# Both down projections of an FFN block in 1 MB units with seven products, the first sum of weight blocks made by an accumulating DMA

## What is computed

```python
def swiglu(x, w_gate, w_up, w_down):
    return (jax.nn.silu(x @ w_gate) * (x @ w_up)) @ w_down

f = swiglu(rmsnorm(h, ffn1_pre_g[l]), ffn1_w_gate[l], ffn1_w_up[l], ffn1_w_down[l])
h = h + 0.5 * rmsnorm(f, ffn1_post_g[l])
```

## Time and profile before

| | us |
|---|---|
| median of 3 runs (1766.72 to 1767.81) | 1766.88 |
| the profiled execution | 1766.51 |
| its span, first to last instruction | 1764.7 |
| PE busy | 1738.4 |
| DVE busy | 1392.2 |
| ACT busy | 961.4 |
| POOL busy | 141.1 |

### The profile page before, as it was taken

How to read it: one execution, slowest core, us unless ns; L and a number is a source line. 1 busy time by engine, 2 the same in 40 slices (tenths; PEclk the granted TensorE clock), 3 DMA queues, 4 the chain that set the end, 5 groups by cost and what they waited for, 6 DMA issues and landing times.

```text
span 1764.7 us, 21449 instructions
## 1 busy us (share of the span) xinstructions
PE 1738.4 (99%) x7784; PEld 1430.1 (81%) x7784; DVE 1392.2 (79%) x1244; ACT 961.4 (54%) x955; POOL 141.1 (8%) x129
## 2 busy tenths in 40 slices
PE   8999999999999999999999999999999999999997
PEld 6878888888888888788888878788888888878886
DVE  6889898989867687755686468888898888858786
ACT  6655555555554454656654446555555555645453
POOL 5100000000000000100000007000000000000000
PEclk9999999999999999999999999999999999999999
DMA  7777777777565567666565657787777777557564
GB/s 230 231 227 219 219 235 219 229 221 216 186 230 191 197 209 262 191 204 174 162 199 168 203 166 249 226 228 215 229 227 226 223 219 223 202 183 226 183 219 182
DMA packets 150616, 372.74 MB, mean 211 GB/s; under 512 B 11404, under 2 KB 13588, under 8 KB 149524
## 3 DMA queue, kind: packets, MB, share of 16 engines
q1 hardware_dynamic: 139284, 351.37, 61.2%
q0 software_dynamic: 11232, 20.45, 7.4%
q10 hardware_dynamic: 32, 0.01, 0.0%
HBM read 367.60 MB, written 4.19 MB: 211 GB/s over the span
## 4 chain that ended last, share of the span: by engine, by line
PE 82%; DMA 8%; DVE 6%; issue 2%; ACT 1%; POOL 0%; DVEq 0%; SPq 0%; ACTq 0%
PE ps L1619 15%; PE ps L1621 15%; PE ps L1620 15%; PE ps L1517 12%; PE ps L1519 11%; PE ps L1518 11%; DMA u_raw<-in_ffn_w_up 6%; DMA u_raw<-in_ffn_w_gate 2%; DVE u_lo L1126 2%; DVE w_lo L1011 1%; PE ps L1614 1%; DVE tsum L1137 1%; PE ps L1826 0%; ACT w_hi L656 0%; PE ps L1553 0%
## 5 line engine op out<-in xcount | busy, mean ns | idle before, releaser
L1011 DVE TENSOR_TENSOR w_lo<-raw,w_hi 128x1024 fp32r<-128x1024 f32 x244 | 306.2, 1262 | 205.3 <-ACT w_hi L656 203.2
L656 ACT CAST w_hi<-raw 128x1024 fp32r<-128x1024 f32 x248 | 258.9, 1052 | 268.7 <-PE ps L1519 205.9
L755 ACT CAST u_hi<-u_raw 128x2048 fp32r<-128x2048 f32 x160 | 305.8, 1911 | 153.9 <-DMA u_raw<-in_ffn_w_up 73.5
L1126 DVE TENSOR_TENSOR u_lo<-u_raw,u_hi 128x2048 fp32r<-128x2048 f32 x160 | 364.1, 2286 | 9.3 <-ACT u_hi L755 5.3
L1619 PE MATMUL ps<-u_hi,xT_hi 128*128 128x512 f32 x648 | 252.5, 390 | 0.4 <-DVE act_g L1163 0.4
L1621 PE MATMUL ps<-u_hi,xT_lo 128*128 128x512 f32 x648 | 252.3, 389 | 0.0
L1620 PE MATMUL ps<-u_lo,xT_hi 128*128 128x512 f32 x648 | 252.1, 389 | 0.0
L1517 PE MATMUL ps<-w_hi,hT_all 128*128 128x512 f32 x544 | 212.5, 391 | 3.0 <-DVE w_lo L1011 3.0
L1519 PE MATMUL ps<-w_hi,hT_all 128*128 128x512 f32 x544 | 211.7, 389 | 0.0
L1518 PE MATMUL ps<-w_lo,hT_all 128*128 128x512 f32 x544 | 211.7, 389 | 0.0
L762 ACT CAST t_hi<-tsum 128x1536 fp32r<-128x1536 f32 x78 | 115.7, 1484 | 147.9 <-DVE tsum L1139 88.5
(11 more groups left out here) (195 smaller groups left out, 2714.0 us busy)
## 6 DMA issues: line engine op xcount, KB each, us to landing
raw<-in_ffn_w_down SPq DMA_DIRECT2D x104, 512.0 KB, 4.6
u_raw<-in_ffn_w_gate SPq DMA_DIRECT2D x42, 1024.0 KB, 5.1
u_raw<-in_ffn_w_up SPq DMA_DIRECT2D x40, 1024.0 KB, 5.1
raw<-in_w_in SPq DMA_DIRECT2D x80, 512.0 KB, 3.8
d_raw<-in_ffn_w_down SPq DMA_DIRECT2D x36, 1024.0 KB, 5.3
u_raw<-in_ffn_w_up SPq DMA_DIRECT2D x80, 256.0 KB, 4.0
u_raw<-in_ffn_w_up SPq DMA_DIRECT2D x40, 512.0 KB, 3.7
u_raw<-in_ffn_w_gate SPq DMA_DIRECT2D x76, 256.0 KB, 3.9
```

The costliest lines, as they stand in the source:

```text
L656: sc.copy(w_hi[:, s], raw[:, s]).then_inc(hi_ready, 1)
L755: sc.copy(unit(u_hi, p), unit(u_raw, p)).then_inc(unit_hi, 1)
L1011: ve.tensor_tensor(w_lo[:, s], raw[:, s], w_hi[:, s].bitcast(f32), ALU.subtract).then_inc(lo_ready, 1)
L1126: ve.tensor_tensor(unit(u_lo, p), unit(u_raw, p), unit(u_hi, p).bitcast(f32), ALU.subtract).then_inc(unit_lo, 1)
```

## The change

All 2048 columns now go through units. Columns 0 to 1023 are 22 units g = 0 to 21 (row pairs 0 to 21 in order), of which 8, 10, ..., 18 have seven products. Columns 1024 to 2047 are 18 units g = 22 to 39, in the order of row pairs 20, 21, 5, 4, 7, 6, ..., 19, 18; the even row pairs 4 to 18 have seven products, with the same forms as in the first half. The last groups (`down_last`) take row pairs 0 to 3. The sum B11 + B12 is made by POOL's accumulating DMA, as in the up stage: `down_pair` is gone, `down_pairs` is new on POOL, and SP loads a seven-product unit in three DMAs, B12 first. The banks of the first half are turned by four, so that its finished sums stand in banks 0 to 3. There are two sets of rests (`rest_of`), one for each half, with additions to the banks of both. The forms are made from the float32 hidden values in 4 instructions of 128x1024 in place of 8, all after the last transposes, and the low parts of hidden blocks 2 and on follow them. The gain is loaded in two halves, the second after the last seven-product unit, now unit 39. In the up stage `t_hi` gets a second buffer.

```diff
+    NU = GF + DU
+    KK = list(range(GF)) + [GF - 2, GF - 1]
+    for k in range(SLOTS, GF - 2, 2):
+        KK += [k + 1, k]
+    DS = tuple(g for g, k in enumerate(KK) if k % 2 == 0 and (8 if g < GF else SLOTS) <= k < GF - 2)
...
+        def d_bank(g, n):
+            return bank(n if g >= GF else (n + 4) % 8)
...
+                for g in range(NU):
+                    if g < 4:
+                        sync.wait_ge(unit_used, unit_count(f, (0, HALVES - 1), 4 + g))
+                    else:
+                        sync.wait_ge(d_used, d_count(f, g - 4))
+                    if g == DS[ND - NF_D - 1] + 4:
+                        load_gain((f1_post, f2_post)[f], 0, 2 * W)
+                    first = 2 * W * (g // GF)
+                    k, b = GK * KK[g], d_raw[d_place(g)]
+                    if g in DS:
+                        sync.dma_start(b[:, B12], w_down[:, k + 1, first + W:first + 2 * W]
+                                       ).then_inc(d_b12[DS.index(g) % 2], 16)
+                        sync.dma_start(b[:, B21:B22 + 1].rearrange("p n c -> p (n c)"),
+                                       w_down[:, k, first:first + 2 * W]).then_inc(d_full[g % 4], 16)
+                        sync.dma_start(b[:, B11], w_down[:, k + 1, first:first + W]).then_inc(d_full[g % 4], 16)
...
+            def down_pairs(f):
+
+                for g in DS:
+                    n, first = DS.index(g) % 2, 2 * W * (g // GF)
+                    pool.wait_ge(d_b12[n], d_pairs(f, g))
+                    pool.dma_start(d_raw[d_place(g)][:, B12], ffn_w[f][2][:, GK * KK[g] + 1, first:first + W],
+                                   accum_op=ALU.add).then_inc(d_pair[n], 16)
...
+                for n in range(2 * TOK):
+                    pair_copy(f, (0, HALVES), n, M5 + n)
+                down_hi(f, 4)
+                for n in range(4):
+                    form_hi_of_down(f, n)
+                for p in range(5, DS[0]):
+                    hidden_hi(f, p - 1)
+                    down_hi(f, p)
...
                 hidden_lo(f, 0)
+                down_lo(f, 0)
+                bank_sums(f, last, range(2))
                 hidden_lo(f, 1)
...
                 down_lo(f, 1)
...
+                bank_sums(f, last, range(2, EVAC))
+                pair_hidden(f, last, 0)
+                pair_hidden(f, last, 1)
+                down_lo(f, 2)
+                down_lo(f, 3)
+                for n in range(4):
+                    down_form(f, n)
+                down_lo(f, 4)
+                hidden_lo(f, 2)
...
+                for g in DS[:ND - NF_D]:
+                    down_sums(f, g)
+                    down_lo(f, g)
+                    down_sums_lo(f, g)
+                    down_lo(f, g + 1)
+                    hidden_lo(f, g // 2 + 1)
+                down_lo(f, GF - 2)
+                down_rest(f, 0)
+                down_lo(f, GF - 1)
+                down_lo(f, GF)
+                for c in range(2):
+                    for t in range(TOK):
+                        add_rest(f, t, c)
+                down_lo(f, GF + 1)
+                for c in range(2):
+                    for t in range(TOK):
+                        gain_bank(2 * f, c, t)
+                down_lo(f, GF + 2)
+                for g in DS[ND - NF_D:]:
+                    down_sums(f, g)
+                    down_lo(f, g)
+                    down_sums_lo(f, g)
+                    if g < NU - 1:
+                        down_lo(f, g + 1)
...
-                ve.tensor_tensor(b[:, B12], b[:, B11], b[:, B12], ALU.add).then_inc(d_pair, 1)
...
+                pe.wait_ge(hT_out, ROUNDS * (f + 1) - 2 * TOK)
+                for g in range(GF):
+                    if g % 2 == 0:
+                        pe.wait_ge(hT_lo_done, FC * f + g // 2 + 1)
+                    down_unit(f, g)
+                    if g == 1:
                         for n in range(2 * TOK):
                             pair_transpose(f, (0, HALVES), n, M5 + n)
...
+                pe.wait_ge(rest_ready, 8 * f + 4)
+                for g in range(GF, NU):
+                    down_unit(f, g)
+                down_last(f, Place(down), None if f else 1)
```

More of the change, by code:

```diff
@@ L351, in d_loaded, with d_pairs @@
         def d_loaded(f, p):
-            return 16 * (f * len(range(p % 4, DU, 4)) + p // 4 + 1)
+            loads = [32 if g in DS else 16 for g in range(p % 4, NU, 4)]
+            return f * sum(loads) + sum(loads[:p // 4 + 1])
+        def d_pairs(f, g):
+            return 16 * ((ds_count(f, g) - 1) // 2 + 1)
         def d_count(f, p):
-            return DU * f + p + 1
+            return NU * f + p + 1
         def ds_count(f, p):
@@ L478, in ffn @@
[L478 to L488, removed]
@@ L1344, in add_rest, with down_rest, total @@
-            def add_rest(f, t, c):
-                pl = Place(starts[f"down{f + 1}"] + 2 * GF)
-                dve.wait_ge(rest_ready, 4 * (f + 1))
-                if c == 2:
+            def down_rest(f, pair):
+                def total(n):
+                    return d_bank(GF * pair, n)
+                done = 8 * f + 4 * pair
+                n11, n12, n21, n22 = (rest_of[pair][:, t, n] for t in range(TOK) for n in range(2))
+                dve.wait_ge(n1_out, 2 * f + pair + 1)
+                dve.wait_ge(n6_done, 2 * f + pair + 1)
+                ve.tensor_tensor(n12, total(N6), n11, ALU.add).then_inc(rest_ready, 1)
+                dve.wait_ge(n7_done, 2 * f + pair + 1)
+                dve.wait_ge(rest_ready, done + 1)
+                ve.tensor_tensor(n21, n12, total(N7), ALU.subtract).then_inc(rest_ready, 1)
+                ve.tensor_tensor(n12, total(N5), n12, ALU.subtract).then_inc(rest_ready, 1)
+                dve.wait_ge(rest_ready, done + 2)
+                ve.tensor_tensor(n22, total(N5), n21, ALU.subtract).then_inc(rest_ready, 1)
@@ L1759, in plain @@
                 def plain(n, x1, b1, x2, b2):
[L1760 to L1765 removed]
+                    three(d_bank(g, n), x1, *b1, first, False)
+                    last = three(d_bank(g, n), x2, *b2, False, last_of_pair)
+                    if last_of_pair:
+                        last.then_inc(pair_done, 1)
@@ L1791, in down_unit @@
-                last = three(bank(N6), form(S2), *sum_of(U2), first, end)
+                if g == DS[0]:
+                    pe.wait_ge(hT_out, ROUNDS * (f + 1))
+                    pe.wait_ge(d_form_lo, 4 * (f + 1))
+                elif first:
+                    pe.wait_ge(fg_done, TOK * NC * 2 * f + 2 * TOK)
+                last = three(d_bank(g, N1), a11, *b11, first, end)
+                if end and g > GF:
+                    last.then_inc(n1_done, 1)
+                three(d_bank(g, N2), a12, *b21, False, False)
```

339 lines of the change are left out of this document (149 added, 190 removed).

## The result

| | before | after |
|---|---|---|
| median, us | 1767.08 (1766.72 to 1767.81, 4 runs) | 1754.08 (1752.99 to 1754.87, 4 runs) |
| profiled execution, us | 1766.51 | 1754.87 |
| its span, us | 1764.7 | 1753.1 |
| PE busy, us | 1738.4 | 1727.7 |
| DVE busy, us | 1392.2 | 1416.0 |

What follows compares the result with a forecast made beforehand. TensorE, busy for 99% of the span, was taken as the bound; -8.16 us of matmuls and -3.6 of waits, all else 0, made -11.8 us, so 1755.1 us, with 8 in 10 from 1753.5 to 1762.5.

Steps and rivals of the forecast that it cites:

- Matmuls, -8.16: Both down projections: 1032 matmuls become 1014 in each, 36 fewer at 0.2267 us on TensorE's path, -8.16 us.
- The two waits of the old chunks, -3.6: Old column chunks: TensorE's two waits for w_lo in each projection go, -3.6 us; 0 if something as late replaces them.
- VectorE, 0: Down stage's first half: VectorE's work fills 9.3 of 10.2 us a pair; cost 0, at most 0.5 us a pair.
- The accumulating DMA, 0: Seven-product units: the accumulate lands after 8.5 us, with 2.3 us of cover and 0.7 more until TensorE waits; cost 0.
- the rival: Accumulate late in every seven-product unit: costs beyond 3.0 us of delay, all gain gone at 8.5 us length; chance 0.07.
- The Trainium skill's rule of the ports that VectorE holds: Accumulate's issue: a GpSimd DMA's descriptor writing stalls during some VectorE instructions; forecast to cost nothing here, by the trace.
- The start of the stage, 0: Down stage's first units: thinnest cover 2.1 us, at unit 4; cost 0, or 1 to 3 us a projection if late.
- The turn, 0: Between column pairs, units 21 and 22: bank additions and gains stand between plain units' splits and fit; cost 0.
- The end, 0: Last chunk's loads behind the gain in SP's queue: some 5 us to the cast, cost 0; with 8.6, 0.6 a projection.
- Second t_hi, 0: Up stages: ScalarE waits less for TensorE, but TensorE's waits there are for u_lo, behind an accumulate; gain 0.
- The sum: Whole kernel: -8.16 - 3.6 = -11.8 us, giving 1754.7 for the profiled execution and 1755.1 us for the median.

Runs made afterwards that it cites:

- plain_first: The changed kernel with only plain units in the first 22, so as many matmuls as the kernel before; 1761.40 us, ratio 0.9970.
- dve_adds: The changed kernel with VectorE adding B11 to B12 itself and no accumulating DMA in the down stages; 1755.43 us, ratio 0.9936.
- single_t_hi: The changed kernel with one t_hi buffer, as before the change; 1755.72 us, ratio 0.9937.
- single_t_hi_again: The changed kernel with one t_hi buffer, run once more beside the changed kernel on one chip; 1755.31 us, ratio 0.9935.
- changed_again: The changed kernel itself, unedited, run once more beside its variants on one chip; 1754.56 us, ratio 0.9933.
- no_acc: The changed kernel without the down stages' accumulating DMAs, B12 alone standing where the sum should; 1751.78 us, ratio 0.9914.

## Why the prediction was right, point by point

*Matmuls, -8.16.* Right: plain_first has the matmuls of before without its waits, and its stages are 4.08 and 4.05 us longer, 8.13 together.

*The two waits of the old chunks, -3.6.* Right in kind, small by 0.5. A projection gains 2.06 us and not 1.8. The 0.16 us between bracket and lost start, taken from the larger wait, holds for the smaller one too (0.56 for 0.40); what the sum left out is that the matmul behind each of them is late as well, by 0.08 and 0.11. Nothing as late took their place in the down stage. One wait of 0.75 us did come up in the mixer, which the forecast didn't have.

*VectorE, 0.* Right: 9.4 us from sum to sum before it waits for TensorE, of 10.2 (forecast 9.3). That it was close is shown by dve_adds: 0.69 us more a pair brings back 1.4 and 1.9 us a projection. The forecast's 0.5 us a pair in 12 pairs, 6 us, was not reached even then.

*The accumulating DMA, 0.* The cost was right, and each step too: 3.3 us to POOL's issue (3.3 to 3.4), landed 8.0 us after the last matmul start of g-4 (8.5), cover 2.7 us (2.3), in the pair shown. VectorE's first sum was released by TensorE 21 times (the line above); the DMA released 2, for 2.0 us together, and TensorE didn't wait for those. That the accumulate always went 2 us ahead of the next load, though, was not part of the forecast's reasoning: the cost of 0 leaned in part on luck. What was wrong is the sentence on the rival, that it decides from 3.0 us of delay and for an accumulate of 8.5 us. It took the length of the accumulate as fixed, from the up stages' 4.0 to 5.7. But the length depends on when the accumulate is issued against SP's next load: in the changed kernel it goes 2.1 us ahead, and if POOL's issue slipped by those 2.1 us it would be 7 us long and cost 25 us. The true margin is thus under 2.1 us, not 3.0, and the drop behind it is steep. It is not under 1.1: in the traces of single_t_hi and single_t_hi_again one accumulate each went only 1.1 us ahead of the load, and one in changed_again 1.5; they took 4.1, 4.2 and 3.7 us, and the stages kept their 209.9. That the accumulate would land in 4 to 6 us (3.6 to 4.4 measured) erred on the safe side.

The Trainium skill's rule of the ports that VectorE holds (SBUF — State Buffer, section "SBUF: two separate sides") was a rival's ground; the section states it for instructions in a 2-port performance mode, such as a copy of float32. The trace shows nothing of it: all 28 issues took 862 to 875 ns beside a VectorE busy for 82% of the stage, nearly all of it with tensor_tensor, so here it cost 0, as the forecast had it.

*The start of the stage, 0.* Right. The last form of the four ends at 497.3, hidden block 2 at 500.64, T + 21.8 with T = 478.81, for T + 21.4 forecast and T + 23.5 needed.

```profile
499.42 1.22 DVE L1138 TENSOR_TENSOR hT_all<-hT,hT_all 128x1024 fp32r<-128x1024 f32 x1
```

*The turn, 0.* Right, no wait of TensorE.

*The end, 0.* Right. Answering, SP's loads of the last chunk, which now stand behind the gain, and the first cast of it:

```profile
689.25 2.19 SPq L444 DMA_DIRECT2D raw<-in_ffn_w_down  x4
...
694.99 1.05 ACT L680 CAST w_hi<-raw 128x1024 fp32r<-128x1024 f32 x1 [8.46 <-DMA raw<-in_ffn_w_down]
```

5.7 us, where the 5 of the forecast and the 8.6 of before were the ends. With the cast and the split that is 697.3, wanted at 688.68 + 10.9 = 699.6.

*Second t_hi, 0.* The term of the sum that missed most: the traces point to -1 to -2 us, with the size not settled. The reason given, that TensorE's waits there are for u_lo, holds for the largest of them; it left out that ScalarE's order also holds VectorE's other work, which the wait for act_g points to.

*The sum.* In the profiled executions -12.25 in the down stages, -1.45 in the up stages, -0.22 in the first chunk and +0.79 in the mixer make -13.1, for the -13.04 by which the last matmul starts earlier. Forecast were -11.8. Of the difference 0.5 is the ring's waits; the other 0.9, the net of the up stages, the first chunk and the mixer, is no larger than what one up stage varies by (420.2 to 422.6), so that the total came so close is in part luck.

## What to carry to other kernels

Where TensorE is busy for 99%, count matmuls and price them by the distance of their starts, then add the waits that go: here that gave 12.2 of the 13 us. All else in such a change is a list of covers to be checked. A cover on a DMA is worth only as much as the DMA's length is known: find what is issued next to it, for a delay within its cover can move it beside another transfer and double its length. And move an addition from VectorE to an accumulating DMA only where VectorE has less than that much left in a pair; here it paid 3.3 of 13 us, by the stages.

## What the runs showed of the hardware

An accumulating DMA of 256 KB that POOL issues within 0.5 us of a plain load of 1 MB takes 6.4 to 8.5 us; 2 us ahead of it 3.6 to 4.4, 2 us behind it 3.9 to 5.5 (up to 4.9 when ahead, in the other kernels that have it there). What grows is the time to its first packet, from 1.6 to 4.4 and 4.8 us; once begun, the packets take the same 1.6 to 1.8 us. Why they stand behind the load's was not separated.

TensorE, idle for 6.1 us, began again at 0.43 us a matmul and not at 0.2267 (granted clock 0.66 in the stretch of the pause and the eight matmuls, 1.00 behind it), so that this wait cost 1.6 us more than its length, and the 28 of that kernel 61.5 us. In no other kernel here was a wait of TensorE for d_lo longer than 2.8 us, and the clock of their down stages stayed at 1.00.

A DMA taken away altogether (no_acc, the DMA engines' busy share from 0.74 to 0.61) left the stage as it was, 209.88 and 209.85 us.
